# A Mamba-2 layer with a mixture of experts: the vector engine's order around the router, the layer-norm rows and two plain weight units

## What is computed

```python
mod = silu(c) @ ada_w + ada_b                 # 6 rows of 1024: sh1 sc1 g1 sh2 sc2 g2
y = ssd_mixer(x * (1 + sc1) + sh1, ...)       # Mamba-2, 4 groups of 8 heads of 64, state 128
x = layer_norm(ALPHA * x + (1 + g1) * y, ln1_g, ln1_b)
hin = x * (1 + sc2) + sh2
eid, wts = route(hin, router_w, router_b)     # softmax over 16, best of 4 groups, best 2 experts in it
y = moe_ffn(hin, eid, wts, w_up, w_down)      # 16 experts: (silu(gate) * up) @ w_down, width 1024
x = layer_norm(ALPHA * x + (1 + g2) * y, ln2_g, ln2_b)
# inside ssd_mixer, per group:
y = scan(...) + d_skip * xs                   # the skip term
y = rms_norm(y * silu(z)) * norm_g            # then @ w_out
```

## Time and profile before

| | us |
|---|---|
| Runs without the profiler: median of 3 | 1172.5 (1170.88 to 1173.53) |
| The profiled execution: its own time | 1168.81 |
| The profiled execution: span from first to last instruction | 1166.7 |
| DVE busy | 940.1 (81%) |
| PE busy | 1027.9 (88%) |
| ACT busy | 628.2 (54%) |
| POOL busy | 493.8 (42%) |

### The profile page before, as it was taken

The page is one execution under the profiler, slowest core; times in us unless marked ns, Lnnn a source line. Parts: engine busy times, 40 slices in busy tenths (PEclk is TensorE's granted clock), DMA queues, the critical chain, the costliest instruction groups (busy, mean ns, idle before and its releaser), DMA issues.

```text
span 1166.7 us, 15729 instructions
## 1 busy us (share of the span) xinstructions
PE 1027.9 (88%) x5234; PEld 842.1 (72%) x5234; DVE 940.1 (81%) x1005; ACT 628.2 (54%) x584; POOL 493.8 (42%) x308
## 2 busy tenths in 40 slices
PE   0798899999988997975899999999999999999960
PEld 0577679777977986845688887788777788878850
DVE  6687973995598377876788989888998898998868
ACT  1354452445236335244477677776776667777640
POOL 1343544544464344201726534355354654446210
PEclk9899989999999998977899999999999999999995
DMA  9232423432451334335789999999999999999963
GB/s 363 64 117 76 146 72 115 138 90 85 127 166 54 96 123 168 132 117 211 279 319 364 369 351 357 356 374 353 349 359 352 370 354 362 366 359 371 361 253 145
DMA packets 101755, 279.39 MB, mean 239 GB/s; under 512 B 9961, under 2 KB 57233, under 8 KB 84319
## 3 DMA queue, kind: packets, MB, share of 16 engines
q1 hardware_dynamic: 95850, 270.65, 64.0%
q0 software_dynamic: 4496, 8.19, 2.0%
q10 hardware_dynamic: 1382, 0.21, 0.1%
HBM read 274.51 MB, written 12.58 MB: 246 GB/s over the span
## 4 chain that ended last, share of the span: by engine, by line
DVE 20%; DMA 19%; PE 13%; issue 10%; ACT 6%; POOL 1%; DVEq 0%; SPq 0%; ACTq 0%; POOLq 0%
DVE moe_r L1172 10%; DMA moe<-in_moe_w_down 9%; DMA moe<-in_moe_w_up 9%; ACT moe_r L781 5%; DVE moe L1279 1%; PE ps L1713 1%; PE ps L1717 1%; PE ps L1715 1%; DVE moe_r L1285 1%; DVE moe_r L1273 1%; PE ps L1424 1%; PE ps L1426 1%; PE ps L1425 1%; PE ps L1665 1%; PE ps L1664 1%
## 5 line engine op out<-in xcount | busy, mean ns | idle before, releaser
L1172 DVE TENSOR_TENSOR moe_r<-moe,moe_r 128x2048 fp32r<-128x2048 f32 x192 | 444.0, 2332 | 67.5 <-ACT moe_r L781 66.2
L781 ACT ACTIVATE moe_r<-moe 128x2048 fp32r<-128x2048 f32 x192 | 368.1, 1921 | 178.0 <-DMA moe<-in_moe_w_up 101.8
L1713 PE MATMUL ps<-moe_r 128*128 128x512 f32 x768 | 224.8, 401 | 19.7 <-DVE both L968 12.0
L1715 PE MATMUL ps<-moe_r 128*128 128x512 f32 x768 | 218.9, 394 | 0.0
L1717 PE MATMUL ps<-moe_r 128*128 128x512 f32 x768 | 218.0, 393 | 0.0
L500 POOL TENSOR_TENSOR ssd_r<-ssd,ssd_r 128x1024 fp32r<-128x1024 f32 x56 | 138.2, 2469 | 142.1 <-ACT ssd_r L625 137.3
L1713 PEld LDWEIGHTS ps<-moe_r 128*128 128x128 f32 x768 | 140.3, 190 | 53.1 <-DVE both L968 12.0
L1717 PEld LDWEIGHTS ps<-moe_r 128*128 128x128 f32 x768 | 145.7, 190 | 31.6
L1715 PEld LDWEIGHTS ps<-moe_r 128*128 128x128 f32 x768 | 145.7, 190 | 31.5
L578 POOL DMA_INDIRECT ydram<-moe,moe_i x16 | 35.4, 2213 | 260.9 <-DVE moe L1291 236.2
L1424 PE MATMUL ps<-ssd_r 128*128 128x512 f32 x320 | 133.4, 417 | 11.6 <-DVE ssd L916 9.8
(11 more groups left out here) (284 smaller groups left out, 1520.0 us busy)
## 6 DMA issues: line engine op xcount, KB each, us to landing
moe<-in_moe_w_up SPq DMA_DIRECT2D x128, 1024.0 KB, 6.7
moe<-in_moe_w_down SPq DMA_DIRECT2D x64, 1024.0 KB, 8.2
ssd<-in_ssd_w_in SPq DMA_DIRECT2D x40, 512.0 KB, 3.9
ssd<-in_ada_w SPq DMA_DIRECT2D x30, 512.0 KB, 3.5
ssd<-in_ssd_w_out SPq DMA_DIRECT2D x16, 512.0 KB, 3.5
ssd<-in_ada_w SPq DMA_DIRECT2D x4, 1024.0 KB, 9.7
early<-in_ada_w SPq DMA_DIRECT2D x4, 1024.0 KB, 11.6
moe<-ydram SPq DMA_DIRECT2D x8, 512.0 KB, 5.2
```

The source lines that it names most:

```text
L781: act.activation(wr[:, i % RING, 0, :], ring[:, i % RING, :], ACT.Identity).then_inc(s_wh, 1)
L1172: dve.tensor_tensor(wr[:, i % RING, 1, :], ring[:, i % RING, :], wr[:, i % RING, 0, :].bitcast(F32), ALU.subtract).then_inc(s_wl, 1)
L1713: mm(to[i], xh, wh[i], start=start, stop=False)
L1715: mm(to[i], xh, wl[i], start=False, stop=False)
```

## The change

Seven edits, told as what they do.

1. **Skip term first.** `gate` is cut in two: `skip(g, q)` (the skip term, L1010 before) and `gate(g, q)` (the product, L1012 before). `skip(g, 0)` and `skip(g, 1)` stand ahead of both gates and no longer wait for silu(z). ACT makes silu in two instructions of two quarters each, with a semaphore count for each.
2. **Layer-norm rows folded by ACT and PE.** `fold_rows` leaves DVE. ACT makes 16 diagonal tiles of 128x128 (`fold_diagonals`) out of the columns `rowa`, `rowb`, PE multiplies them with a tile of ones in four matmuls of 512 columns (`fold_row`), and ACT copies the four results out of PSUM (`fold_copy`).
3. **First expert's first unit later.** `low(0, 0)` leaves the middle of the residuals; `high(0, 0)` and `high(0, 1)` on ACT come behind the exponential of the softmax, and so do `normalise(2)` and `normalise(3)`. The square roots (`deviation`) stand by themselves, ahead.
4. **`sel` before the weights.** DVE makes the positions and `sel` directly behind the mask, ahead of weights and table.
5. **Units 2 and 3 of the first expert are used as plain float32** (`PLAIN`): no `high`, no `low`, four float32 matmuls of 512 columns each on `xfull` and the ring's slot. SP's loads into these slots wait for PE (`s_wu`) instead of DVE.
6. **All four `modulate(t)` come after the first expert's rows**, and `gate_row(G - 1)`, `low(0, 0)` and `low(0, 1)` come ahead of them. SP's stores to `h2d` and its loads of units 6 and 7 behind them wait for those.
7. **`slots(1)` comes behind `low(0, 5)`**, and PE's `slot_rows(1)` behind unit 4.

The diff, cut to its core:

```diff
...
           ebc.rearrange("p s t -> p (s t)"), place(D, state_at)]
-foldtmp = place(D, state_at + D)
+diag = [place(D, state_at + D).rearrange("p (k n) -> p k n", k=DC),
+        seg.rearrange("p s c t -> p (s c t)").rearrange("p (k n) -> p k n", k=DC)]
 rwall = xw.rearrange("p c n -> p (c n)")
...
 mod_bank = lambda k: 0 if k < 4 else 7
+fold_bank = (0, 4, 1, 0)
+PLAIN = (2, 3)
 wo_bank = lambda i: (0, 1, 4)[i % 3]
...
                 sp.dma_start(h2d[t * P:(t + 1) * P, :], oacc[:, t, :]).then_inc(ld_h2, 16)
-        sp.wait_ge(s_wl, moe_unit(0, i, True) - RING + 1)
+        sp.wait_ge(s_wu if i - RING in PLAIN else s_wl, moe_unit(0, i, True) - RING + 1)
         load_up(0, i)
...
         act.wait_ge(s_zc, ZT * (g + 1))
-        act.activation(yT, yT, ACT.Silu).then_inc(s_zs, 1)
+        for j in range(2):
+            act.activation(yT[:, 2 * j:2 * j + 2, :], yT[:, 2 * j:2 * j + 2, :], ACT.Silu).then_inc(s_zs, 1)
         if not last:
...
-    def normalise(t):
+    def deviation(t):
...
         act.activation(rstd[:, t:t + 1], mv[:, t, 1:2], ACT.Sqrt, bias=epsc).then_inc(s_sd1, 1)
+    def fold_diagonals():
+        act.wait_ge(s_rwp, 1)
+        act.wait_ge(s_yz, 4 * G)
+        act.wait_ge(s_y, 4 * G)
+        for a, col in enumerate((rowa, rowb)):
+            for k in range(DC):
+                op = act.activation(diag[a][:, k, :], ident, ACT.Identity, scale=col[:, k:k + 1])
+            op.then_inc(s_diag, 1)
+    def fold_copy(i):
+        act.wait_ge(s_rws, 2 + i)
+        n = i % 2
+        act.activation(modr[:, 2 - i // 2, n * 512:(n + 1) * 512], bank(fold_bank[i]), ACT.Identity).then_inc(s_fold, 1)
+    def normalise(t):
         act.wait_ge(s_shift, t + 1)
...
     act.sem_inc(s_hTh, 2)
+    fold_diagonals()
     for h in range(TT + 1):
         half_rows(h)
+    deviation(0)
     normalise(0)
     half_rows(TT + 1)
+    deviation(1)
     normalise(1)
-    high(0, 0, True)
     half_rows(TT + 2)
-    normalise(2)
+    deviation(2)
+    fold_copy(0)
     half_rows(TT + 3)
-    normalise(3)
-    high(0, 1, True)
+    deviation(3)
+    fold_copy(1)
...
     act.activation(prob, prob, ACT.Exp).then_inc(s_ex, 1)
-    high(0, 2, True)
+    normalise(2)
+    normalise(3)
+    high(0, 0, True)
+    high(0, 1, True)
+    fold_copy(2)
+    fold_copy(3)
+    act.wait_ge(s_wh, AHEAD + 2)
+    act.sem_inc(s_wh, len(PLAIN))
     act.wait_ge(s_nrm, TT)
...
     act.activation(xe[:, 0, 4:8, :], xfull[:, 4:8, :], ACT.Identity).then_inc(s_xeh, 1)
-    high(0, 3, True)
-    act.wait_ge(s_fold, 3)
+    act.wait_ge(s_fold, 4)
     act.activation(lnr, lnr, ACT.Identity, scale=ALPHA).then_inc(s_fold, 1)
...
-    def gate(g, q):
+    def skip(g, q):
...
         dve.scalar_tensor_tensor(yt, xT[:, q, :], gnd[:, 1, q:q + 1], bank(6 + q % 2), ALU.mult, ALU.add).then_inc(s_y1, 1)
+    def gate(g, q):
+        yt = seg[:, q % 2].rearrange("p c t -> p (c t)")
+        dve.wait_ge(s_zs, 2 * g + q // 2 + 1)
         dve.wait_ge(s_y1, 4 * g + q + 1)
...
         dve.wait_ge(s_m, HG * g + HG)
-        dve.wait_ge(s_zs, g + 1)
+        skip(g, 0)
+        skip(g, 1)
         gate(g, 0)
...
             xbc_tile(g + 1, 1)
+        skip(g, 2)
         gate(g, 2)
+        skip(g, 3)
         gate(g, 3)
...
-    def fold_rows():
-        dve.wait_ge(ld_ln, 16 * 2)
-        dve.tensor_tensor(foldtmp, lnr[:, 1, :], modr[:, 2, :], ALU.mult).then_inc(s_fold, 1)
-        dve.wait_ge(s_fold, 1)
-        dve.tensor_tensor(modr[:, 1, :], foldtmp, modr[:, 1, :], ALU.add).then_inc(s_fold, 1)
-        dve.tensor_tensor(modr[:, 2, :], lnr[:, 0, :], modr[:, 2, :], ALU.mult).then_inc(s_fold, 1)
     def modulate(t):
         dve.wait_ge(s_nrm, t + 1)
+        dve.wait_ge(s_fold, 4)
         link(dve.tensor_tensor(h2f[t], xt[:, t, :], modr[:, 2, :], ALU.mult))
...
     scale(1)
-    low(0, 0, True)
     residual(1, 3)
...
     scale(3)
-    fold_rows()
     dve.wait_ge(s_lg, 2 * TT)
...
     op.then_inc(s_mask, 1)
+    dve.wait_ge(s_pos, 1)
+    link(dve.scalar_tensor_tensor(pm, ps[:, 7, 0:TT * E].rearrange("p (t e) -> p t e", e=E), 1.0, mask, ALU.add, ALU.mult))
+    link(dve.tensor_scalar(tab[:, :, 0:E, 4], pm, -1.0, None, ALU.add))
+    for t in range(TT):
+        op = dve.tensor_scalar(sel[:, t, :], iota, tab[:, t, 0, 4:5], None, ALU.is_equal)
+    op.then_inc(s_sel, 1)
     link(dve.tensor_tensor(wts, prob, mask, ALU.mult))
...
     dve.tensor_copy(tab[:, :, 0:E, 2], whi.bitcast(F32))
-    dve.tensor_tensor(tab[:, :, 0:E, 3], wts, whi.bitcast(F32), ALU.subtract)
-    dve.wait_ge(s_pos, 1)
-    link(dve.scalar_tensor_tensor(pm, ps[:, 7, 0:TT * E].rearrange("p (t e) -> p t e", e=E), 1.0, mask, ALU.add, ALU.mult))
-    link(dve.tensor_scalar(tab[:, :, 0:E, 4], pm, -1.0, None, ALU.add))
+    link(dve.tensor_tensor(tab[:, :, 0:E, 3], wts, whi.bitcast(F32), ALU.subtract))
     dve.tensor_copy(tabc[:, :, 0:5], tab[:, :, 0, :]).then_inc(s_tabc, 1)
-    dve.wait_ge(s_tabc, 1)
-    for t in range(TT):
-        op = dve.tensor_scalar(sel[:, t, :], iota, tabc[:, t, 4:5].bitcast(F32), None, ALU.is_equal)
-    op.then_inc(s_sel, 1)
...
     dve.tensor_scalar(nblk_i[0:1, 1:2], nbf[0:1, 1:2], float(E - 1), None, ALU.add).then_inc(s_nblk, 1)
+    gate_row(G - 1)
+    low(0, 0, True)
     low(0, 1, True)
-    for t in range(3):
-        modulate(t)
+    dve.wait_ge(s_wl, AHEAD + 2)
+    dve.sem_inc(s_wl, len(PLAIN))
...
     def moe(b, first, last):
-        for i in range(3, 6):
+        for i in range(4 if first else 3, 6):
             low(b, i, first)
-            if first and i == 4:
-                slots(1)
+        if first:
+            slots(1)
         if not first:
...
     dve.tensor_tensor(xe[:, 1, 4:8, :], xfull[:, 4:8, :], xe[:, 0, 4:8, :].bitcast(F32), ALU.subtract).then_inc(s_xel, 1)
-    modulate(3)
+    for t in range(TT):
+        modulate(t)
     slots(0)
-    low(0, 2, True)
-    gate_row(G - 1)
     dve.wait_ge(s_bcu, 2 * G + 1)
...
         op.then_inc(s_lg, 1)
+    def fold_row(i):
+        if i == 3:
+            pe.wait_ge(s_fold, 1)
+        else:
+            pe.wait_ge(s_oacc, 8 * (G - 1) + 1 + (7, 6, 8)[i])
+        pe.wait_ge(s_diag, i // 2 + 1)
+        n = i % 2
+        mm(bank(fold_bank[i]), ones, diag[i // 2][:, 4 * n:4 * n + 4, :].rearrange("p k n -> p (k n)"), start=True, stop=True).then_inc(s_rws, 1)
...
         half_logits(5)
+        fold_row(0)
+        fold_row(1)
         half_turned(7)
...
         half_logits(7)
+        fold_row(2)
+        fold_row(3)
...
                 pe.wait_ge(s_hid, 2 * b + 2)
+            if first and i in PLAIN:
+                pe.wait_ge(ld_w[i % RING], moe_loads(b, i, first))
+                for n in range(4):
+                    op = mm(bank(n), xfull[:, i, :], ring[:, i % RING, n * 512:(n + 1) * 512], start=False, stop=False)
+                op.then_inc(s_wu, 1)
+                continue
             pe.wait_ge(s_wl, moe_unit(b, i, first) + 1)
...
                 turn_hidden(b - 1)
-            if first and i == 3:
+            if first and i == 4:
                 pe.wait_ge(s_xel, 2)
...
         op.then_inc(s_xgt, 1)
+    pe.wait_ge(s_tabc, 1)
     slot_rows(0)
     pe.wait_ge(s_bcu, 2 * G + 1)
+    pe.wait_ge(s_fold, 4)
     moe(0, True, False)
...
```

4 lines of the change are left out of this document (2 added, 2 removed).

## The result

| | before | after |
|---|---|---|
| Four runs, median (lowest to highest), us | 1172.34 (1170.88 to 1173.53) | 1139.38 (1131.71 to 1145.67) |
| The profiled execution: own time, span, us | 1168.81, 1166.7 | 1145.67, 1143.9 |
| Mean granted TensorE clock | 0.953 | 0.971 |
| DVE, PE busy, us | 940.1, 1027.9 | 932.0, 1020.6 |

Ratio 0.9716, 95% interval 0.9655 to 0.9778: the change is faster by 33 us (26 to 40), against a forecast of 29.1 by its sum and 1143.4 us for the time. The profiled execution of after is the slowest of its four.

The account below looks back on a forecast made before the run. Bounds taken: PE in the SSD loop, DVE's list from 494 to 565 us, a nearly full load queue in the expert loop. 7.5 + 6.5 + 0.9 + 14.2 = 29.1 us off 1172.5 gave 1143.4 us, range 1138 to 1147.

Parts of the forecast that it names:

- Term 1: Groups 0 to 2: skip first puts DVE's gate 1 ahead of POOL, shortening PE's wait; 2.5 us a turn, 7.5 us.
- Term 2: Groups 0 to 2: PE keeps full clock behind the gap before tile 4; 6.5 us, bounds nothing to 6.5.
- turns of about 98.6 us: Sign that the forecast is right: the length of a turn of the group loop after the change.
- Term 3: Group 3: DVE's wait at the skip term goes, 0.9 us; ACT's 16 diagonals cost nothing, uncovered up to 1 us.
- Term 4: Way to the router: low(0, 0), fold_rows and part of the square-root wait leave DVE; router's first instruction 9.7 us earlier.
- Terms 4 and 5: From the residuals over the router to the first expert's slots(2): together 14.2 us earlier, taken from 13.2 to 15.2.
- rival B: First expert gives back its early start, units 6 and 7 or expert 1's gather late; 1147.8 us, chance 0.10.
- term 5: Mask to first expert: PE starts that expert at 521.2 us, not 541.01; slots(2) at 549.6 to 551.6, not 564.78.
- Rival A: Groups: POOL still takes the SBUF port first, only 0.91 us a group gained; 1154.7 or 1148.2 us, chance 0.18.
- C: Expert loop: the load queue is the bound and eats the earlier start; 1172.5 us, chance 0.03.
- D: Expert loop: new PE gaps lose the clock, 2.56 us in each of 14 experts; slower, 1179 us, chance 0.05.
- E: One part does nothing, as the skip term if ACT's or POOL's order holds DVE; 1158.3 us, chance 0.06.

Follow-up runs that it names:

- a_again: The changed kernel, no edit, profiled a second time: 1137.8 us, ratio 0.9726 to the kernel before.
- c_noskip: The changed kernel without the skip-first part (one silu, DVE waits for all of it before skip and gate): 1153.0 us, ratio 0.9854 to the kernel before.
- d_silu_whole: The changed kernel with silu in one instruction again, skip products still first: 1140.1 us, ratio 0.9741 to the kernel before.
- b_skip: The kernel before with only the skip products first and the silu in two: 1154.4 us, ratio 0.9876 to the kernel before.
- f_low0: The changed kernel with high(0,0) and low(0,0) put back among the residuals: 1151.3 us, ratio 0.9801 to the kernel before.
- h_slots: The changed kernel with slots(1)'s rows made ahead of unit 2 and unit 6's load ahead of the last h2 store: 1141.1 us, ratio 0.9716.
- g2_split: The changed kernel with the first expert's units 2 and 3 split again instead of plain float32: 1144.1 us, ratio 0.9775 to the kernel before.
- n_more: h_slots plus POOL's selection before its gather, low(1,0) before slots(2), low(1,2) and high(1,2) later, first expert's selection behind the weights: 1135.2 us, ratio 0.9697.

## Why the prediction was right

Its sum was 29.1 us. The measured medians differ by 33.0 us and, for a_again and the runs of before beside it, by 32.1, with 29.1 inside both intervals. Step by step:

- **Term 1**, the skip first, 2.5 us a turn: 2.84 by c_noskip's turn at full clock, 2.73 to 2.74 by the waits of the kernel before itself, so 8.2 to 8.5 in all for 7.5. The step that undersized it is "I take 2.5 us of the 2.74 a turn": all of PE's wait went.
- **Term 2**, the clock, 6.5 us: the turns gave 15.14, less 8.2 to 8.5 is 6.6 to 6.9. It was right in size, by luck: the clock behind one and the same wait is lost in one turn and kept in another, as c_noskip shows, where it cost 3.9 us in all instead. The bounds "nothing to 6.5" say this better than the sum. The sign "turns of about 98.6 us" doesn't follow from the terms: these give 99.8 for the first two turns, and 99.5 and 99.4 were measured.
- **The mechanism of both** held: gate 1 went ahead of POOL and took 0.64 us, not 2.40. The sentence of the Trainium skill ("SBUF — State Buffer", section "Who interferes with whom") on issue order is borne out: 2.40 and 2.23 us behind POOL's unit in before and c_noskip, 0.64 ahead of it. The margin, 0.6 us between the start of gate 1 and POOL's, was near the 0.5 forecast. The credit for silu's halves ("first silu half done near 352.8") was misplaced: d_silu_whole has the whole gain without them, since the whole silu is through 0.5 us before the second skip term is.
- **Term 3**, 0.9 us: b_skip's way to the router is 1.33 us shorter, and c_noskip's 1.1 longer. The diagonals cost nothing that can be seen: they take ACT 4.8 us in a_again, and it still waits 2.17 us for PE ahead of the first half-row copy (6.85 in the kernel before). No version takes them out alone.
- **Term 4**, 9.7 us to the router: from b_skip to a_again 59.50 - 50.15 = 9.35. In the first profile it was 8.2: PE waits 4.93 us early in group 3 in both, and then stayed at half clock a microsecond or two longer in the first (mean of the next 10 us 0.71, against 0.83 in a_again). DVE's list divides the 9.35. The last residual starts 5.2 us earlier (5.3 forecast). From there to the last reciprocal, behind ACT's square root, it is 5.37 us in b_skip and 4.06 in a_again: 1.3 (0.9 forecast). From the reciprocal to the router it is 3.81 and 0.94: 2.9, where 3.5 was forecast for the fold; the step that was mis-sized left out that DVE, without the fold, waits 0.58 us for the logits. The prediction also missed what `low(0, 0)` did to PE. In the kernel before, PE stood 6.69 us for the residual behind it and ran at half clock from there (0.50 from 502 to 508 us):

```profile
502.32 1.12 PE L1537 MATMUL ps<-both,moe 128*128 128x128 f32 x4 [6.69 <-DVE moe L998]
```

The fold on DVE hid that: PE had finished the logits at 507.0 us, and the router started behind the fold at 509.24. With the fold gone it would have cost 1.6 us, as f_low0 shows (7.0 us at the router for 5.4 on DVE). The prediction priced PE's work there at full clock without saying why it should be so, and was right since the wait went with `low(0, 0)`.
- **Terms 4 and 5**, 14.2 us at slots(2): the way from the last silu to slots(2) was 114.78 in b_skip, 100.77 in after and 98.90 in a_again, so 14.0 and 15.9. The chain from slots(1) over POOL's selection and PE to slots(2) was there as forecast, slots(2) 9.13 and 9.99 us behind slots(1), for 10.3. But slots(1) alone didn't rule it: h_slots made it 5.9 us earlier and POOL then waited for the last store of h2. The prediction's reason against its rival B, slack at unit 6, said nothing of the gather's wait for that store, and h_slots leaves it hardly any slack.
- **Within term 5** the gather was rightly put behind PE's modulation rows, and 0.8 us of wait for the positions was right too (0.93). PE's wait ahead of unit 4 was forecast at 2.2 us, with the clock lost half the time: it was 1.96 and 1.97, and the clock was lost in the first profile (L1760 at 1.91 us) and kept in the second. A plain unit took 3.5 us, not 3.7. That the selection's move brings nothing stood in these numbers, but the text did not say it. What the plain units are worth was not priced singly; g2_split makes it 6.1 us, of some 6.5 that came behind the router.

Rival A fell with gate 1's time. B fell: from the router's 9.35 us the second expert had 15.9. C and D fell with the last column of the table: the loop takes 588 to 599 us from any start, before's 592.70 among them, at a clock of 1.00. E fell for the skip term, though two pieces of the change (the halves, the selection's move) show no gain.

The profiled execution alone would have said 23 us. The marks between say 30.7 us in the first profile and 32.7 in a_again, near the 33.0 and 32.1 of the medians. The 8 us between 23 and 30.7 are the prologue's and the loop's scatter, 3.2 and 4.8 us, and no term was wrong by that much.

## What to carry to other kernels

A wait for something that an instruction doesn't need costs its own length, and more if it hands a shared port to another engine: here 0.9 us of wait became 2.8 us, and then, in most turns, a slow clock on a third engine. Where a move on one engine shortens another's wait, look at the clock behind that wait too: a unit among the residuals cost 5.4 us on DVE and 1.6 more in PE's clock. When a list on DVE rules a stretch, judge a move by what waits at its end: selecting rows early did nothing because PE's queue was full, and plain float32 products, slower on PE, were worth 6 us because they took work from DVE. Where executions scatter by more than a piece is worth, measure between marks in the profile, with the stretches that the edit can't reach left out.

## What the runs showed beyond that

**The clock in the prologue differs from one execution to the next.** The prologue is the same code in all fourteen profiles, and the first silu comes anywhere from 141.83 to 146.18 us. PE's tile there in a_again:

```profile
83.60 0.80 PE L1455 MATMUL ps<-ssd_r 128*128 128x512 f32 x1 [1.60 <-DVE ssd L948]
...
84.62 0.63 PE L1457 MATMUL ps<-ssd_r 128*128 128x512 f32 x1
85.05 0.63 PE L1455 MATMUL ps<-ssd_r 128*128 128x512 f32 x1
```

and in n_more:

```profile
83.16 0.50 PE L1463 MATMUL ps<-ssd_r 128*128 128x512 f32 x1 [0.91 <-DVE ssd L955]
...
83.98 0.40 PE L1463 MATMUL ps<-ssd_r 128*128 128x512 f32 x1
```

With a wait of 1.60 us the tile runs at 1.2 GHz (a matmul every 0.43 us), with 0.91 at 2.4 (0.23). But b_skip and g2_split have the same wait of 1.60 us there and keep the full clock (1.00 from 82 to 92 us). From 82 to 92 us the granted clock was 0.66 in six profiles, and the first silu came at 145.93 to 146.18 in all six; in the other eight it was 0.83 to 1.00 and the silu at 141.83 to 144.99. So 1.60 us can be enough to lose the clock or not, and 2.81 us can be too little: the length of the wait alone doesn't decide it.

**And so does the port's price.** In after, POOL and DVE start within 0.02 us of each other, and DVE's addition takes 2.92 us:

```profile
61.14 2.40 POOL L503 TENSOR_TENSOR ssd_r<-ssd,ssd_r 128x1024 fp32r<-128x1024 f32 x1 [4.83 <-ACT ssd_r L628]
```

```profile
61.16 2.92 DVE L1150 TENSOR_TENSOR ssd<-ssd 32x512 f32<-32x512 f32 x1
```

In a_again POOL started at 60.42, 1.78 us ahead of the addition, which then took 1.16. In before DVE started at 61.25, 1.60 us ahead of POOL, and took 0.68. So how far POOL is ahead sets the price. Between before and after that was PE's clock one tile earlier (a granted clock of 0.80 from 50 to 56 us in before, 1.00 in after), behind which ACT hands POOL its part; in a_again the clock had been lost still earlier (0.66 from 40 to 50 us, 0.83 in after). What makes one execution of the same program differ from another in the first place, and what makes the loop take 588 us in one and 599 in the next, stays open; nothing here was made to find it.
